# Attention stage of a hybrid diffusion trunk: head norms per column on GpSimd, softmax combination in one pass, convolution work moved out of the attention loop

## What is computed

```python
u = h @ w_in                                    # q, k, v, convolution, Fourier columns
s = einsum('bhiqd,bhikd->bhiqk', q, k) * HEAD_DIM ** -0.5    # i = 0, 1: two softmaxes a head
p = softmax(s); p_diff = p[:, :, 0] - lam * p[:, :, 1]
o = rmsnorm(p_diff @ v, g_subln) * (1 - lam_init)            # norm over the 128 values of a head
y = a * sigmoid(gate); y = depthwise_conv31(y) + b_dw
y = silu(layernorm(y)) @ w_pw + b_pw
f = real(fft2(u_f)) @ w_f + b_f
x = x + gate * (concat(o, y, f) @ w_out)
```

## Time and profile before

| | |
|---|---|
| median of 3 runs | 2882.47 us (2881.99 to 2888.78) |
| the profiled execution | 2883.3 us, its span 2881.4 us |
| busy share of the span | PE 95%, PEld 80%, DVE 60%, ACT 27%, POOL 6% |
| mean granted TensorE clock | 0.977 of full speed |
| instructions of POOL | 136 |

### The profile page before, as it was taken

The page is one execution under the profiler, slowest core; times in us unless marked ns, Lnnn a source line. Parts: engine busy times, 40 slices in busy tenths (PEclk is TensorE's granted clock), DMA queues, the critical chain, the costliest instruction groups (busy, mean ns, idle before and its releaser), DMA issues.

```text
span 2881.4 us, 37801 instructions
## 1 busy us (share of the span) xinstructions
PE 2730.6 (95%) x15288; PEld 2307.6 (80%) x15288; DVE 1731.1 (60%) x2338; ACT 784.4 (27%) x1078; POOL 177.6 (6%) x136
## 2 busy tenths in 40 slices
PE   6999999999986999999999999999999977899998
PEld 4888888879844778888888788888888845888887
DVE  5655656574967475655656756565445866544445
ACT  4212111132156431112112411111224156322222
POOL 1000000030010210000000200000011011200001
PEclk7999999999999999999999999999999989999999
DMA  7532333312001123332322223333121101133221
GB/s 265 177 116 87 112 107 102 103 45 74 30 30 59 45 70 121 102 102 90 129 88 88 83 93 106 112 101 102 44 88 59 45 30 59 59 104 101 87 88 44
DMA packets 180753, 255.32 MB, mean 89 GB/s; under 512 B 5310, under 2 KB 128812, under 8 KB 180652
## 3 DMA queue, kind: packets, MB, share of 16 engines
q1 hardware_dynamic: 180652, 253.90, 27.3%
HBM read 251.78 MB, written 2.10 MB: 88 GB/s over the span
## 4 chain that ended last, share of the span: by engine, by line
PE 87%; DVE 6%; ACT 3%; POOL 2%; issue 1%; SPq 1%; DMA 0%; ACTq 0%; DVEq 0%; POOLq 0%
PE ps L860 27%; PE ps L861 27%; PE ps L862 27%; PE ps L1125 1%; POOL sqsum L851 1%; PE ps L1205 1%; PE ps L1233 1%; DVE e L2017 1%; DVE nb L2027 1%; DVE h_lo L1681 1%; ACT e L1542 1%; PE ps L1001 1%; ACT w_hi L1311 1%; PE ps L1219 1%; PE ps L1174 1%
## 5 line engine op out<-in xcount | busy, mean ns | idle before, releaser
L860 PE MATMUL ps<-h_hi,w_hi 128*128 128x512 f32 (+1 forms) x3040 | 1044.6, 344 | 10.9 <-DVE h_lo L1681 9.3
L861 PE MATMUL ps<-h_lo,w_hi 128*128 128x512 f32 (+1 forms) x3040 | 1041.3, 343 | 0.0
L862 PE MATMUL ps<-h_hi,w_lo 128*128 128x512 f32 (+1 forms) x3040 | 1039.8, 342 | 0.0
L860 PEld LDWEIGHTS ps<-h_hi,w_hi 128*128 128x128 f32 x3040 | 579.7, 191 | 81.5 <-issue 9.7
L861 PEld LDWEIGHTS ps<-h_lo,w_hi 128*128 128x128 f32 x3040 | 579.7, 191 | 66.0 <-issue 1.0
L862 PEld LDWEIGHTS ps<-h_hi,w_lo 128*128 128x128 f32 x3040 | 579.2, 191 | 66.0
L1780 DVE TENSOR_TENSOR prod<-sil,ps 128x512 f32<-128x512 f32 (+1 forms) x156 | 88.0, 568 | 638.4 <-PE ps L862 630.5
L860 PE MATMUL ps<-hid_hi,w_hi 128*128 128x512 f32 (+1 forms) x1248 | 432.9, 347 | 0.0
L861 PE MATMUL ps<-hid_lo,w_hi 128*128 128x512 f32 (+1 forms) x1248 | 429.2, 344 | 0.0
L862 PE MATMUL ps<-hid_hi,w_lo 128*128 128x512 f32 (+1 forms) x1248 | 429.0, 344 | 0.0
L1311 ACT ACTIVATE w_hi<-raw 128x2048 fp32r<-128x2048 f32 x158 | 297.0, 1906 | 474.5 <-PE ps L862 474.5
(11 more groups left out here) (138 smaller groups left out, 1959.2 us busy)
## 6 DMA issues: line engine op xcount, KB each, us to landing
side_raw<-in_w_ada SPq DMA_DIRECT2D x120, 512.0 KB, 3.7
raw<-in_w_ffn_gate SPq DMA_DIRECT2D x44, 1024.0 KB, 5.3
raw<-in_w_ffn_up SPq DMA_DIRECT2D x44, 1024.0 KB, 5.3
raw<-in_w_ffn_down SPq DMA_DIRECT2D x44, 1024.0 KB, 4.9
raw<-in_w_in SPq DMA_DIRECT2D x14, 1024.0 KB, 5.3
ada_buf<-in_w_ada SPq DMA_DIRECT2D x9, 1024.0 KB, 10.5
raw<-in_w_out SPq DMA_DIRECT2D x8, 1024.0 KB, 6.7
raw<-in_w_in SPq DMA_DIRECT2D x8, 512.0 KB, 4.7
```

The costliest lines, as they stand in the source:

```text
L860: mm(out, wh, xh, start=start, stop=False)
L861: mm(out, wh, xl, start=False, stop=False)
L862: return mm(out, wl, xh, start=False, stop=stop)
```

## The change

What it does:

- **Column norms.** The value product is turned round (`pT` is the stationary operand), so that a unit's output has query rows on partitions. `take_o` (DVE) copies it to `onorm`, `square_o` (ACT) sums its squares per row, `head_scale` (POOL) makes the inverse root of that sum by a seed and three Newton rounds in columns of one element a partition, and scales `onorm`. `turn_o` (PE) transposes it back, six steps after the unit's scores (`OT_LAG`), and `head_high` (ACT) and `head_low` (DVE) make its two parts, the low one in `a_lo`. PE waits for `o_scaled` at the head of its step. The last three units are turned inside the out product.
- **One-pass combination.** DVE forms one ratio per row and adds the second exponential times it to the first; the division by the first sum is left to the head norm.
- **The convolution's norm and pointwise product** leave the attention loop and stand in the Fourier stretch (`conv_mean`, `conv_var`, `conv_spread`, `point_wise`), with `conv_scales` on POOL between the second and the third.
- **Order of the front.** PE does K first, then convolution, Q, V, Fourier columns (`keys_first`). DVE's ropes of K stand first and the taps are spread between `w_lo` tiles and the ropes of Q. ACT copies the latent part of K from PSUM.
- **POOL** has the units' norms in order, and makes the low halves of `out` tiles 0 to 2 after units 3, 6 and 9. Its other splits are of K tiles where they were of V tiles.

```diff
+T_LAG, O_LAG, OT_LAG = 2, 3, 6
...
+            def conv_scales(l):
+                nt = sum(n for _, n in mix_segs(l)) // 128
+                x, y, t = cvar[:, 0:nt], nt_y[:, 0:nt], nt_t[:, 0:nt]
+                wait_freed(pool, ("var", l))
+                step(ts(y.bitcast(I32), x.bitcast(I32), -0.5, SEED, ALU.mult, ALU.add))
+                for _ in range(3):
+                    settle()
+                    step(ptt(t, y, y, ALU.mult))
+                    settle()
+                    step(ptt(t, t, x, ALU.mult))
+                    settle()
+                    step(ts(t, t, -0.5, 1.5, ALU.mult, ALU.add))
+                    settle()
+                    step(ptt(y, y, t, ALU.mult))
+                settle()
+                for i in range(nt):
+                    ts(diag[:, i, :], ident[:], nt_y[:, i:i + 1], None, ALU.mult).then_inc(diag_ready, 1)
...
+            def head_scale(l, u):
+                i = u % 8
+                x, y, t = nt_x[:, i:i + 1], nt_y[:, i:i + 1], nt_t[:, i:i + 1]
+                s0 = esum[:, i, 0:1]
+                pool.wait_ge(osq_done, units_before(l) + u + 1)
+                step(ts(t, s0, s0, EPS, ALU.mult, ALU.mult))
+                settle()
+                step(ts(x, osq[:, i:i + 1], 1.0 / 128, t, ALU.mult, ALU.add))
+                settle()
+                step(ts(y.bitcast(I32), x.bitcast(I32), -0.5, SEED, ALU.mult, ALU.add))
+                for n in range(3):
+                    settle()
+                    step(ts(t, y, y, x, ALU.mult, ALU.mult))
+                    settle()
+                    step(ts(t, t, -0.5, 1.5, ALU.mult, ALU.add))
+                    settle()
+                    if n < 2:
+                        step(ts(y, y, t, None, ALU.mult))
+                    else:
+                        step(ts(oscale[:, i:i + 1], y, t, None, ALU.mult))
+                settle()
+                ts(onorm[:, u % 4, :], onorm[:, u % 4, :], oscale[:, i:i + 1], None, ALU.mult).then_inc(o_scaled, 1)
             for q in range(3 * DEPTH + 1):
...
-                    attention_help(q // 3)
+                    conv_scales(q // 3)
+                    for u in range(len(units_of(q // 3))):
+                        head_scale(q // 3, u)
+                        if u in (3, 6, 9):
+                            split(("out", q // 3, (3, 6, 9).index(u)))
...
+            def turn_o(l, u):
+                wait_bank(pe, ("OT", l, u))
+                pe.wait_ge(o_scaled, units_before(l) + u + 1)
+                nc.tensor.transpose(ps[:, 6, 0:128], onorm[:, u % 4, :], ident[:]).then_inc(products, 1)
...
-                                pe.wait_ge(mix_ready, HEADS * sum(len(mix_segs(x)) for x in range(l)) + k * ns + s + 1)
+                                if k == HEADS - 1 and s == 0:
+                                    for u in late_units(l):
+                                        turn_o(l, u)
+                                wait_freed(pe, ("OT", l, last_unit(l, k, s)))
+                            x_lo = a_lo if k < HEADS else h_lo
...
+                    if 0 <= i - OT_LAG < len(us):
+                        turn_o(l, i - OT_LAG)
...
-                        if t == ms[s][1] // 128 - 1:
-                            last.then_inc(products, 1)
-                    if 0 <= i - 2 < len(us) and us[i - 2][1] == 0:
+                            last = mm(ps[:, 7, 0:128], pT[:, u % 2, k if s == 0 else k - 4, :],
+                                      vN[:, k, 128 * h:128 * h + 128], start=(k == ks[0]), stop=(k == 5), skip_group_check=True)
+                        last.then_inc(products, 1)
...
+                def square_o(u):
+                    wait_freed(act, ("O", l, u))
+                    if u_before + u >= 2:
+                        act.wait_ge(osq_done, u_before + u - 1)
+                    act_fn(ojunk[:, u % 2, :], onorm[:, u % 4, :], ACT.Square, accum_out=osq[:, u % 8:u % 8 + 1]).then_inc(osq_done, 1)
...
+                def head_high(u):
+                    h, s, t = us[u]
+                    o = ms[s][0] + 128 * t
+                    wait_products(act, ("OT", l, u))
+                    act_fn(h_hi[:, h, o:o + 128], ps[:, 6, 0:128], ACT.Copy, scale=gsub[:, l:l + 1]).then_inc(head_hi_done, 1)
...
-                    step(dve_.reciprocal(rs[:, p, :], sums[:, p, :]))
+                    c, n = ratio[:, i % 8:i % 8 + 1], TOK if s == 0 else CTX
+                    step(dve_.reciprocal(rs[:, i % 2, 1:2], esum[:, i % 8, 1:2]))
                     settle()
-                    step(dve_.tensor_scalar(e1[:, p, 0:n], e1[:, p, 0:n], rs[:, p, 1:2], neglam[:, l:l + 1], ALU.mult, ALU.mult))
+                    step(dve_.tensor_scalar(c, rs[:, i % 2, 1:2], esum[:, i % 8, 0:1], neglam[:, l:l + 1], ALU.mult, ALU.mult))
                     settle()
-                    stt(out=e0[:, i % 3, 0:n], in0=e0[:, i % 3, 0:n], scalar=rs[:, p, 0:1], in1=e1[:, p, 0:n],
+                    stt(out=e0[:, i % 3, 0:n], in0=e1[:, i % 2, 0:n], scalar=c, in1=e0[:, i % 3, 0:n],
                         op0=ALU.mult, op1=ALU.add).then_inc(p_ready, 1)
...
+                def take_o(u):
+                    wait_products(dve, ("O", l, u))
+                    dve_.tensor_copy(onorm[:, u % 4, :], ps[:, 7, 0:128]).then_inc(bank_free[7], 1)
...
+                def head_low(u):
+                    h, s, t = us[u]
+                    o = ms[s][0] + 128 * t
+                    dve.wait_ge(head_hi_done, u_before + u + 1)
+                    stt(out=a_lo[:, h, o:o + 128], in0=ps[:, 6, 0:128], scalar=gsub[:, l:l + 1],
+                        in1=h_hi[:, h, o:o + 128].bitcast(F), op0=ALU.mult, op1=ALU.subtract).then_inc(bank_free[6], 1)
...
+                for i in range(len(us) + OT_LAG):
+                    if 0 <= i - OT_LAG < len(us):
+                        head_low(i - OT_LAG)
                     if i < len(us):
...
+                        maximum(i)
                     if 1 <= i <= len(us):
                         combine(i - 1)
...
+                    if 0 <= i - O_LAG < len(us):
+                        take_o(i - O_LAG)
...
+                conv_mean()
...
+                    if j == 0:
+                        conv_var()
+                conv_spread()
...
+                point_wise()
...
+                split(("conv", l, 0))
+                dve.wait_ge(tables_landed, 48)
+                rotate_k(0)
+                rotate_k(1)
+                split(("conv", l, 1))
+                rotate_k(2)
+                rotate_k(3)
+                split(("Q", l, 0))
+                glu(0)
+                for i in range(4):
+                    tap(0, i)
+                split(("Q", l, 1))
+                for i in range(4, 12):
+                    tap(0, i)
+                glu(1)
+                both_taps(0, 4)
+                split(("V", l, 0))
+                both_taps(4, 8)
+                rotate_q(0)
+                rotate_q(1)
+                split(("V", l, 1))
+                both_taps(8, 14)
+                rotate_q(2)
+                rotate_q(3)
+                split(("four", l))
+                both_taps(14, 19)
+                for i in range(19, TAPS):
+                    tap(1, i)
```

More of the change, by code:

```diff
@@ L1107, in fourier, with conv_mean @@
                 ms = mix_segs(l)
+                ns = len(ms)
+                nt = sum(n for _, n in ms) // 128
+                before = 2 * segs_before(l)
                 small = raw_of(("W", l))[:].rearrange("p (i k n) -> p i k n", i=4, k=2)
+                def conv_mean():
+                    pe.wait_ge(acc_ready, 2 * (l + 1))
+                    for s, (o, n) in enumerate(ms):
+                        ao = 0 if s == 0 else C_CTX - HALF
+                        wait_bank(pe, ("mean", l, s))
+                        for c in range(2):
+                            last = mm(pt(("mean", l, s), n), ones[:], acc[:, c, ao:ao + n], start=(c == 0), stop=(c == 1))
+                        last.then_inc(products, 1)
@@ new lines, in point_wise @@
+                def point_wise():
+                    for p in range(2):
+                        for s, (o, n) in enumerate(ms):
+                            ao = 0 if s == 0 else C_CTX - HALF
+                            wait_bank(pe, ("pw", l, p, s))
+                            pe.wait_ge(cs_done, before + 2 * s + 2)
+                            for c in range(2):
+                                last = mm(pt(("pw", l, p, s), n), small[:, 0, c, 128 * p:128 * p + 128], acc[:, c, ao:ao + n],
+                                          start=(c == 0), stop=(c == 1))
+                            last.then_inc(products, 1)
@@ L1179, in attention @@
                 ms = mix_segs(l)
[L1180 to L1181 removed]
+                u_before = units_before(l)
+                e_before = 2 * u_before
                 slots = score_slots(l)
@@ L1559, in mix @@
-                    beside(i)
-                    if i in (3, 4, 14):
-                        split(next(rest))
```

(12 more changed lines are left out.)

617 lines of the change are left out of this document (293 added, 324 removed).

## The result

The changed kernel takes 2911.24 us (median of 4, 2910.10 to 2911.28) against 2882.29 for the kernel before on the same chip: ratio 1.0095, 95% interval 1.0079 to 1.0111. It is slower by about 27 us. The profiled execution has a span of 2909.2 us against 2881.4, 27.8 more.

What follows compares the result with a forecast made beforehand. Attention loops were taken as bound by a ring of waits among PE, DVE and ACT, front and Fourier by PE. Layer 0 +9.9, layer 1 -5.1 and front -2 gave +2.8 on 2883.3: 2886 us, range 2846 to 2940.

Steps and rivals of the forecast that it cites:

- the sum: Whole kernel: layer 0 +9.9, layer 1 -5.1, front -2, together +2.8 us on 2883.3.
- POOL's chain sets the pace: Attention loops: POOL's units at 5.3 (latent) and 4.8 us (context) are slower than PE's steps; chance 0.42.
- the rival of dear small instructions: POOL's norm chain: fetching a scalar column costs 0.10 us more a step, +48 us, 2934 us; chance 0.27.
- The step of 0.34 us: POOL's norm chain: each small instruction takes 0.20 us plus 0.14 waiting on itself, twelve to a unit.
- the rival of cheap small instructions: POOL's norm chain: a step of 0.24 us, units 4.1 and 3.6, 2848 us; chance 0.27 together with no lock.
- The last of the chain at 0.35: POOL's final 128x128 scaling of a unit: between 0.20 and 0.47 us, taken as 0.35.
- The lock: Attention loops: DVE's two-input combination stops POOL's chain for 0.88 us a latent and 0.34 us a context unit.
- POOL's start: Attention loops: POOL begins its first unit 16 us after the first scores in layer 0, 16.3 in layer 1.
- a stall of 3.8: Out product: PE's 9.9 us of matmuls against POOL's 13.7 for three late units and the last turn; layer 0 +2.6.
- Fourier and the fronts: Fourier: convolution work becomes bare PE time, +12.5 and +8.6 us, plus 0.5 in layer 0; fronts: -1 us each layer.
- the ring's step: Attention loop before the change: an undisturbed latent step of scores, transposes and value product on PE, 4.1 us.

Runs made afterwards that it cites:

- the one with short rounds: Changed kernel with each of the three Newton rounds in two POOL instructions instead of three, and a second factor in the last scaling: 2871.34 us.
- the run with one operand: Changed kernel with DVE's combination reading one SBUF operand instead of two, the second softmax left out: 2902.55 us.
- the fastest kernel: Changed kernel with two short Newton rounds, `out` tiles on DVE, the turn in bank 7, and DVE's value-product copy before its combination: 2848.41 us.

## Why the prediction was right, and where its sizes were off

The range of 2846 to 2940 holds 2911, and slower had the largest chance, 0.44; the likeliest time, 2886, was 25 us short and the result lies outside that case's own range. The mechanism of the sum, POOL's chain sets the pace, is shown by the run with four rounds, which changes the chain alone, and by the one with short rounds. What failed are sizes, and one wait that the sum did not have. That the result was inside is in part owed to the width of the range: the sum itself came to +2.8 us, no change, and slower had the largest chance mostly because the rival of dear small instructions was added to it.

*The step of 0.34 us.* Measured 4.29 us for twelve, 0.357 each. It is made up differently: a scalar column costs 0.07 to 0.08 more (0.27 and 0.34 against 0.19), as the rival "dear small instructions" had it with 0.10, and the wait of an instruction on itself is 0.09 to 0.11, not 0.14. The two nearly cancel: +0.2 a unit. So the step of 0.35, from which on the rival ends on the slower side, was passed, by little. (In the rival of cheap small instructions the three terms make -35, which is what 2848 goes with, not -36.)

*The last of the chain at 0.35.* It takes 0.62, more than the upper bound of 0.47, and a wait on itself comes with it that I had left out: +0.36 a unit, the larger error. The bound came from an addition of 256 columns, another form; the run with a second factor shows how much a form matters (0.37).

*The lock.* It is there, and where it strikes it adds 0.72 us, against 0.88 forecast for a latent unit. But it doesn't strike all units: 21 units of layer 0 took 115.4 us without their tiles (840.16 to 969.41, less 13.8), 5.50 each, so 0.50 a unit of lock against 0.73 in the sum; 13 of layer 1 took 5.64. Part of the own chain's error is hidden by this, and that is luck. 5.50 against 5.16 in 21 units is 7.1 of the 8.6 us by which layer 0's loop was missed; in layer 1, missed by 8.4, it is 4.4, and POOL's start, 18.7 us after the first scores and not 16.3, 2.4 more.

The Trainium skill (SBUF — State Buffer, on the engine-side ports) counts a DVE instruction with two SBUF inputs among those that block a GpSimd instruction which reads SBUF. The trace agrees for the combination, 1.34 against 0.62, and for DVE's tiles, 1.95 against 0.27. The same page (the part on who interferes with whom) counts a one-input scaling of SBUF data among the blockers too when it runs in a 2-port mode; my expectation for the run with one operand had left that out. The run agrees that such a scaling blocks and is blocked (0.97 against 0.62 on POOL, 4.54 against 0.62 on DVE); that it ran in such a mode no row says, though it is quicker, 0.62 us for 768 columns in place of 1.02. One thing is open: by the rows POOL's instruction of 0.97 us had begun 0.21 us ahead of DVE's and was stretched all the same.

*"POOL makes three more units", a stall of 3.8.* The out product's excess is 8.2 and 10.3 us instead of 2.6 and 3.8, of which 0.5 and 1.5 are the longer wait for the statistic, and here the mechanism was wrong in one step. ACT, POOL and PE at the end of layer 0's loop:

```profile
970.96 0.29 DVE L2154 COPY onorm<-ps 128x128 f32<-128x128 f32 x1 [0.26 <-PE ps L1338]
...
978.73 0.62 POOL L891 TENSOR_SCALAR onorm<-onorm,oscale 128x128 f32<-128x128 f32 x1
...
981.52 0.37 ACT L1647 ACTIVATE h_hi<-ps,gsub 128x128 fp32r<-128x128 f32 x1 [10.91 <-PE ps L1146]
981.79 0.30 ACT L1640 ACTIVATE ojunk<-onorm 128x128 f32<-128x128 f32 x1
...
982.27 0.27 POOL L875 TENSOR_SCALAR nt_t<-esum 128x1 f32<-128x1 f32 x1 [2.92 <-ACT ojunk L1640]
...
987.33 0.45 PE L1146 MATMUL ps<-ident,onorm 128*128 128x128 f32 x1 [4.67 <-POOL onorm L891]
```

The last unit is in `onorm` at 971.25, and POOL is free at 979.35. But ACT's queue has `head_high` of unit 21 ahead of `square_o` of unit 23, and PE turns unit 21 only in the midst of the out product, at 981.21. So the last chain begins 2.9 us late and is bare. The stall there is one unit's chain less some 0.3 us, however fast POOL is: 4.67 here, 5.8 with four rounds, 3.6 with short rounds, 2.7 with two. `square_o` ahead of `head_high` would free it; this wasn't tried.

*The clock, which the sum left out.* PE's rows and windows around that stall:

```profile
981.00:987.40 6.40, 0.88 (x5) 0.36 (x4) 0.70 (x2) 1.02 (x4) 3.76 (x13) 0.91 0.00 0
987.40:992.00 4.60, 4.60 (x16) 4.02 (x17) 1.85 (x3) 0.37 (x1) 0.00 (x0) 0.50 0.63 213
...
997.00:1002.00 5.00, 5.00 (x25) 4.14 (x24) 3.14 (x3) 3.57 (x5) 1.27 (x1) 1.00 0.00 0
```

```profile
980.98 0.39 PE L925 MATMUL ps<-h_hi,w_lo 128*128 128x512 f32 x1
...
988.43 0.63 PE L925 MATMUL ps<-h_hi,w_lo 128*128 128x512 f32 x1
```

After 6 us in which PE did next to nothing it has a granted clock of 0.50, 1.2 GHz, for about 5 us; the out product's matmuls then start 0.43 us apart instead of 0.23, so a stall of 4.7 us costs some 2 more behind it (4.6 us for what takes 2.5 at 0.23). In layer 0's loop the clock fell from 0.93 to 0.82, but there PE waits for POOL's chain anyway.

*Fourier and the fronts.* +11.9 and +7.8 against +13.0 and +8.6; POOL's thirteen steps and six scalings took 7.2 us (797.27 to 804.47) and lay beside the second half of `Z`. DVE's last tap ended at 765, 18 us ahead of Fourier. The fronts gave 1.7 and 2.0 us, 3.7 together, where the sum had 2. Fourier held; the fronts gave nearly twice what the sum had, each within the 2 us that the prediction allowed.

*What was right for a reason I did not have.* The sum set the loop's new pace against the old one as a whole. The two runs on the kernel before show the parts: one pass instead of two is worth 12 us, and the convolution cost 29 in the loop against 20 outside. If the two gains add up, which no run shows, POOL's chain used up these 21 us and 27 more. What it brought to take the head norms' wide work out of the loop was not measured by itself.

## What to carry to other kernels

Count a serial chain on GpSimd as one queue with a pace of its own. Multiply it by the number of units, and compare it with the ring's step before the code is written: here 5.0 us against about 4.1, and three instructions less in each unit, with a quicker form for the last, turned a loss of 27 us into a gain of 12. To the chain's own length comes what DVE blocks of it, 0.5 us a unit here, and work moved from GpSimd to DVE can come back that way. A wait at the head of an engine's step is only as early as the slowest thing in its producer's queue, so when a lag is introduced, look at the last units apart, where consumers are turned late. And idle time of an engine inside a ring is no room for work that another engine of the ring must finish first.

## What the hardware showed that I had not expected

- A GpSimd scaling of 128x128 by a column takes 0.62 us with one operation and 0.37 with two (the second a constant factor): 40 of them 28.6 against 16.7 us, disturbed ones included.
- A DVE instruction with one SBUF operand stretches a GpSimd one as well (0.62 us on DVE; 0.97 instead of 0.62 on POOL), and stands 4.54 us beside a GpSimd tile of 4.51.
- A GpSimd instruction of one column takes 1.95 us instead of 0.27 beside a DVE tile of 2.28.
- TensorE's busy time depends on its waits. The same 15352 matmul instructions took 2719.3 us in the fastest kernel, 2743.0 in the changed one and 2759.8 in that with four rounds, with a mean clock in layer 0's loop of 0.95, 0.82 and 0.75. This is mostly not time lost: with one round more PE is busy 16.8 us longer, but layer 0's loop grew by 22.6 us, which POOL's 21 units explain alone. The slower matmuls lie inside the waits. Where no wait covers them, as behind the stall above, they cost time.
